# A hybrid decoder step on one Trainium2 core: the first delta chunk's gate rows, differences, exponentials and key products placed around the last projection tile

## The chip, the cores and the metric

The kernel runs as one launch on one core of a Trainium2 chip. The metric is device time in microseconds, from three executions of the kernel before. One more execution was taken with the hardware profiler, and all rows below are from that one.

## The reference, cut to what matters

The program is one inference step of a two-layer decoder trunk, for a prompt of 512 tokens and for 8 sequences of 4 sample tokens (544 columns in all). Each layer has three branches that read the same normalised input; branch A is a gated DeltaNet, and the change lies in it:

```python
c, dn_conv_new = _causal_conv(dn_qkv, dn_conv0, dn_conv_w)
q, k, v = jnp.split(jax.nn.silu(c), [DN_HEADS * DN_DK, 2 * DN_HEADS * DN_DK], axis=-1)
q = _l2norm(heads(q, DN_HEADS)) * DN_DK ** -0.5
k = _l2norm(heads(k, DN_HEADS))
beta = jax.nn.sigmoid(dn_b.astype(F32))
g = -jnp.exp(dn_a_log.astype(F32)) * jax.nn.softplus(dn_a.astype(F32) + dn_dt_bias.astype(F32))
o_a, dn_s_new = _chunked_recurrence(q, k, heads(v, DN_HEADS), g, beta, dn_s0)
```

In each chunk of the recurrence a unit lower-triangular system is solved. Its matrix is built from key products k k^T, from exponentials of differences of the running sums of g, and from beta. The output also needs the products k q^T with the same exponentials. Branch C is a sparse attention. Its sample part reads pages of a cache of keys and, once the probabilities are there, pages of a cache of values.

## The kernel before

The program is written engine by engine: each engine has one function with its instructions in the order in which they run, and semaphores tie the functions together. The same code is run for both layers, so what happens once in it happens twice in the profile. PSUM is split into two wide buffers `PJ[0]` and `PJ[1]` (`big` in the profile) and four banks `X[0]` to `X[3]` (`aux`). `claim` names the next use of a bank and gives the count of `drained` at which the bank is free again; `filled` says that TensorE has written it. All ScalarE operations go through one helper (L1564), so ScalarE's rows are told apart by their tiles.

Two phases matter here. The **projection phase** runs over `DN_PHASE`, 20 tiles p = 0 to 19. A tile is two halves of 8 k-steps with three matmuls each (`dense_tile`, L880 to L882), and in `between()` something may be placed between its halves. Tiles that carry q, k or v of the DeltaNet are then copied out by ScalarE into `d_pad` (with the stored rows), run through a convolution of four operations on VectorE (L2380, L2383) into `d_conv`, and through Silu on ScalarE into `qkv`. `silu_of(11)` is the last of these, for the tile p = 19. In the last tiles the sample attention ends as well: `sample_probabilities` (after p = 18, transposes at L942 into `X[2]`, `X[3]` and `X[0]`), and `new_values` (between the halves of p = 19, L1215, into `X[1]`), which ScalarE copies to `s_new` (the tile `s_ak` in the profile).

The **chunk phase** runs over five chunks, c = 0 to 3 with 128 tokens and c = 4 with the 32 sample tokens. TensorE begins a chunk with four groups of four matmuls: the gate rows `grow` into `X[1]` and `betarow` into `X[0]` (L1285), then the key products `kk` into `X[2]` and `kq` into `X[3]` (L1292). VectorE takes the differences `dif` from `grow` (L2434, into `d_dec`), ScalarE takes the exponential of `d_dec` and, from the bank of `grow`, the exponential `d_eg`, and VectorE goes on to the matrix of the system. TensorE meanwhile goes on with two value pages, the transposes `dvT` into `X[1]`, two more value pages, ten gate steps (a gate step is one k-step of a gate projection, placed here to fill waits), `dkT` and so on.

A value page is a DMA of 256 KB from the cache into one of four buffers. These buffers are the memory of `d_conv` and `d_pad`, so the SP queue waits for the last Silu before it issues the first:

```python
sp.wait_ge(act_out.sem, act_out.at(('silu', 11)))
for i in range(NPAGES):
    if i >= VPAGES:
        sp.wait_ge(pe_out.sem, pe_out.at(('v', i - VPAGES)))
    sp.dma_start(g.vpage[i % VPAGES], page('cache_v', *divmod(i, NPG)))...
```

Of the kernel before, what the change touches and what calls it, by code (L numbers as in the profile page):

```python
# [25 lines left out]
ALU = mybir.AluOpType  # L26
# [3 lines left out]
P = 128  # L30
# [7 lines left out]
H = 4  # L38
# [190 lines left out]
def gate_no(u, i):  # L229

    return int(u[4]) * 8 + int(u[5]) * 2 + i
# [427 lines left out]
def layer_program(g, layer):  # L659
# [218 lines left out]
    def _(pe):  # L878
# [330 lines left out]
        def new_values():  # L1209

            pe.wait_ge(X[0].drained, X[0].at('spT_new'))
            pe.wait_ge(X[1].drained, X[1].claim('s_new'))
            for h in range(H):
                hs = slice(h * NS, h * NS + NS)
                mm = pe.matmul(X[1].ap[hs, 0:P], g.s_pT[0:NS, NPG, hs], g.s_v[:, h * P:h * P + P], start=True, stop=True)  # L1215
            mm.then_inc(X[1].filled, 1)

        for p, (u, j) in enumerate(DN_PHASE):
            def between():
                key_slot(2 * p)  # L1220
                if p in L2_AT:
                    t = L2_AT[p]
                    column_sums(('l2', t), 1 - p % 2, [((lambda: pe.wait_ge(act_out.sem, act_out.at(('l2sq', t)))), g.l2)])
                if p == SELECT_AT:
                    repeat_selection(0)
                    repeat_selection(1)
                if p == SELECT_AT + 3:
                    new_values()
            dense_tile(('gate', gate_no(u, j)) if u in GATES else ('dn', 2 * int(u[2]) + j), p % 2, u, j, g.uhi, g.ulo,
                       between=between)  # L1230
            key_slot(2 * p + 1)
            if p == SELECT_AT:
                repeat_selection(2)
                new_keys()
            if p == SELECT_AT + 2:
                sample_probabilities()
        pe.wait_ge(PJ[0].drained, PJ[0].claim('so'))

# [38 lines left out]
        for c in range(5):  # L1277
            cs, n = chunk_of(c)
            tri = const('triu') if c < 4 else const('triu_s', NS)[:, 0:NS]
            q, k, v = (g.qkv[:, 4 * i:4 * i + 4, cs] for i in range(3))  # L1280
            for bank, key, src, rhs in ((X[1], 'grow', gG, tri), (X[0], 'betarow', gBeta, ident[0:n, 0:n])):
                pe.wait_ge(bank.drained, bank.claim((key, c)))
                x = bank.ap
                for h in range(H):
                    mm = pe.matmul(x[:, h * n:h * n + n], src[0:n, c, h:h + 1].to_broadcast([n, P]), rhs,  # L1285
                                   start=True, stop=True)
                mm.then_inc(bank.filled, 1)
            for bank, key, a, b in ((X[2], 'kk', k, k), (X[3], 'kq', k, q)):
                pe.wait_ge(bank.drained, bank.claim((key, c)))
                x = bank.ap  # L1290
                for h in range(H):
                    mm = pe.matmul(x[0:n, h * n:h * n + n], a[:, h, :], b[:, h, :], start=True, stop=True)  # L1292
                mm.then_inc(bank.filled, 1)
            if c == 4:
# [265 lines left out]
    def _(ac):  # L1560
# [255 lines left out]
        def silu_of(t):  # L1816
# [5 lines left out]
                    act_out.sem, act_out.next(('silu', t)))  # L1822
            ac.wait_ge(act_out.sem, act_out.count)
        ac.wait_ge(vec_out.sem, vec_out.at('d_pads'))
        even_pages(-1)
        for p, (u, j) in enumerate(DN_PHASE):
# [7 lines left out]
            if u in GATES:  # L1834
# [9 lines left out]
                continue  # L1844
            t = 2 * int(u[2]) + j
            pad = g.d_pad[t % 2]
            if t >= 2:
# [20 lines left out]
            if p == SELECT_AT + 1:  # L1868
# [3 lines left out]
                ac.wait_ge(act_out.sem, act_out.count)  # L1872
            if p == SELECT_AT + 3:
                copy_out(X[1], 's_new', lambda x: [(g.s_new, x[:, 0:P])])
        silu_of(11)
# [16 lines left out]
        for c in range(5):  # L1892
            cs, n = chunk_of(c)
            ac.wait_ge(vec_out.sem, vec_out.at(('dif', c)))
            act(g.d_dec[0:n, 0:4 * n], g.d_dec[0:n, 0:4 * n], ACT.Exp).then_inc(act_out.sem, act_out.next(('dec', c)))
            ac.wait_ge(act_out.sem, act_out.count)
            if c:
                ac.wait_ge(X[0].drained, X[0].at(('dS', c - 1)))
            copy_out(X[1], ('grow', c), lambda x: [(g.d_eg[:, 0:4 * n], x[:, 0:4 * n])], f=ACT.Exp)
            if c == 4:  # L1900
# [163 lines left out]
    def _(ve):  # L2064
# [264 lines left out]
        def sample_logits():  # L2329
# [18 lines left out]
            ve.wait_ge(vec_out.sem, vec_out.count)  # L2348

        odd_pages(-1)  # L2350
        for p, (u, j) in enumerate(DN_PHASE):
# [22 lines left out]
            if t is None:  # L2374
                continue
            ve.wait_ge(act_out.sem, act_out.at(('pad', t)))
            if t >= 2:
# [50 lines left out]
        for c in range(5):  # L2428
            cs, n = chunk_of(c)
            tri = const('triu') if c < 4 else const('triu_s', NS)[:, 0:NS]  # L2430
            ve.wait_ge(X[1].filled, X[1].at(('grow', c)))
            x = X[1].ap
            for h in range(H):
                ts(g.d_dec[0:n, h * n:h * n + n], x[0:n, h * n:h * n + n], gC[0:n, c, h:h + 1], 0.0,  # L2434
                        ALU.subtract, ALU.min).then_inc(vec_out.sem, vec_out.next(('dif', c) if h == 3 else None))
                ve.wait_ge(vec_out.sem, vec_out.count)
            ve.wait_ge(act_out.sem, act_out.at(('dec', c)))
# [355 lines left out]
```

## Time and profile before

| what | value |
|---|---|
| median of 3 runs | 3038.18 us (3035.11 to 3042.14) |
| profiled execution, its own time | 3036.19 us |
| profiled execution, span of the trace | 3034.3 us |
| mean granted TensorE clock | 0.955 |
| busy: TensorE, VectorE, ScalarE | 2817.3, 1620.5, 1177.2 us |

A busy time is the sum of an engine's instructions, and says nothing of what the others waited for. A row of the timeline gives the start of a group of like instructions, the time from its first start to its last end, the line, the tiles (output, then inputs) and how many they are. Square brackets hold the time in which that engine was idle just before, and the work that ended this idle time. A matmul of float32 operands in the groups of the chunk phase stands as two instructions, so four matmuls are counted as x8. PEclk 1.00 is TensorE's full clock of 2.4 GHz and 0.50 is 1.2 GHz. Ends of matmuls overlap the next start, so durations on TensorE are best read from start to start.

### The profile page before, as it was taken

The page shows a single profiled execution, that of the slowest core. Times are in us where ns is not written, and L with a number is a line of the kernel's source. Part 1 is how long each engine was busy: PE and PEld are TensorE (multiplying, and loading weights), DVE is VectorE, ACT ScalarE, POOL GpSimd, SP SyncE. Part 2 cuts the span into 40 slices and gives each one's busy share as a digit, 9 for nine tenths or more (in the row PEclk, how much of TensorE's full clock was granted, in tenths as well). Part 3 has the DMA queues.
Part 4 walks back from the last instruction along what each step waited for, and adds up shares of the span by engine and source line. Part 5 has one row for each costly group of instructions (what it writes and reads, how often), then busy time and mean ns, then how long its engine had stood idle before and what let it go on. Part 6 is the DMA issues. An engine that isn't in the chain of part 4 may idle for free. (4 is left out here: it accounts for less than half of the span.)

```text
span 3034.3 us, 56732 instructions
## 1 busy us (share of the span) xinstructions
PE 2817.3 (93%) x22451; PEld 2635.6 (87%) x22451; DVE 1620.5 (53%) x2513; ACT 1177.2 (39%) x2049; POOL 788.7 (26%) x364
## 2 busy tenths in 40 slices
PE   5998999998999799999979989999899979999998
PEld 4998888887887799999968989888888869999997
DVE  2363665564445549558225538546644464781861
ACT  3442333673223533333334315447622343432332
POOL 1221131221002333343322203222200124334431
PEclk8999899999999899999979979999999999999998
DMA  5221333534335432232242223255343344223323
GB/s 173 70 84 51 104 103 96 171 120 123 110 99 178 141 84 80 68 104 80 68 117 70 70 67 99 97 150 159 108 119 104 109 152 151 70 71 104 84 74 95
DMA packets 371700, 316.74 MB, mean 104 GB/s; under 512 B 47726, under 2 KB 321544, under 8 KB 370502
## 3 DMA queue, kind: packets, MB, share of 16 engines
q10 hardware_dynamic: 257332, 188.09, 20.9%
q1 hardware_dynamic: 114098, 124.96, 14.1%
q8 instruction: 181, 2.97, 0.4%
q14 instruction: 89, 0.73, 0.1%
HBM read 276.84 MB, written 36.15 MB: 103 GB/s over the span
## 5 line engine op out<-in xcount | busy, mean ns | idle before, releaser
L873 POOL TENSOR_TENSOR w_lo<-w_raw,w_hi 128x1024 fp32r<-128x1024 f32 (+2 forms) x360 | 788.5, 2194 | 2207.9 <-ACT w_hi L1564 2207.7
L880 PE MATMUL big<-uhi,w_hi 128*128 128x272 f32 x4096 | 1242.3, 303 | 54.0 <-DVE ulo L2084 31.9
L882 PE MATMUL big<-uhi,w_lo 128*128 128x272 f32 x4096 | 1200.6, 293 | 0.0
L881 PE MATMUL big<-ulo,w_hi 128*128 128x272 f32 x4096 | 1195.1, 292 | 0.0
L880 PEld LDWEIGHTS big<-uhi,w_hi 128*128 128x128 f32 x4096 | 788.5, 192 | 108.2 <-issue 60.1
L881 PEld LDWEIGHTS big<-ulo,w_hi 128*128 128x128 f32 x4096 | 789.9, 193 | 4.2 <-issue 1.9
L882 PEld LDWEIGHTS big<-uhi,w_lo 128*128 128x128 f32 x4096 | 787.5, 192 | 0.0
L1564 ACT ACTIVATE w_hi<-w_raw 128x1024 fp32r<-128x1024 f32 (+2 forms) x360 | 343.7, 955 | 425.1 <-PE big L882 329.5
L880 PE MATMUL big<-hhi,w_hi 128*128 128x272 f32 x704 | 205.9, 292 | 3.9 <-DVE hlo L2664 3.9
L882 PE MATMUL big<-hhi,w_lo 128*128 128x272 f32 x704 | 203.5, 289 | 0.0
L881 PE MATMUL big<-hlo,w_hi 128*128 128x272 f32 x704 | 202.7, 288 | 0.0
L1564 ACT ACT_TABLE_LOAD x106 | 136.0, 1283 | 41.7 <-PE big L931 14.3
L2670 DVE TENSOR_TENSOR x<-x,big 128x544 f32<-128x544 f32 x32 | 23.1, 722 | 236.2 <-PE big L882 236.2
L2403 DVE TENSOR_TENSOR d_T<-d_T,aux 128x512 f32<-128x512 f32 (+2 forms) x100 | 62.6, 626 | 144.5 <-PE aux L1342 143.1
L2646 DVE TENSOR_SCALAR f_conv<-f_pad,par 128x560 f32<-128x560 f32 x88 | 136.0, 1545 | 3.1
L880 PEld LDWEIGHTS big<-hhi,w_hi 128*128 128x128 f32 x704 | 132.8, 189 | 5.0 <-DVE hlo L2664 4.3
L881 PEld LDWEIGHTS big<-hlo,w_hi 128*128 128x128 f32 x704 | 132.8, 189 | 0.4
L882 PEld LDWEIGHTS big<-hhi,w_lo 128*128 128x128 f32 x704 | 132.3, 188 | 0.0
L2648 DVE SCALAR_TENSOR_TENSOR f_conv<-f_pad,par,f_conv 128x560 f32<-128x560 f32 x88 | 117.8, 1339 | 3.1
L2383 DVE SCALAR_TENSOR_TENSOR d_conv<-d_pad,par,d_conv 128x568 f32<-128x568 f32 x72 | 106.8, 1483 | 2.6
L1564 ACT ACTIVATE d_y<-aux 128x256 f32<-128x256 f32 (+2 forms) x102 | 38.9, 382 | 171.2 <-PE aux L1328 169.3
L1564 ACT ACTIVATE ffn_last<-f_pad 128x2 f32<-128x2 f32 (+1 forms) x176 | 37.1, 211 | 153.1 <-DVE f_pad L2642 150.0
(360 smaller groups left out, 3905.2 us busy)
## 6 DMA issues: line engine op xcount, KB each, us to landing
w_raw<-in_w_in ACTq DMA_DIRECT2D x66, 1024.0 KB, 5.6
w_raw<-in_w_up ACTq DMA_DIRECT2D x88, 512.0 KB, 5.0
kpage<-in_cache_k SPq DMA_DIRECT2D x128, 256.0 KB, 3.1
w_raw<-in_w_down ACTq DMA_DIRECT2D x32, 704.0 KB, 4.7
d_conv<-in_cache_v SPq DMA_DIRECT2D x64, 256.0 KB, 2.7
d_pad<-in_cache_v SPq DMA_DIRECT2D x64, 256.0 KB, 2.7
gate_dram<-gate_raw ACTq DMA_DIRECT2D x48, 272.0 KB, 2.5
w_raw<-in_w_branch ACTq DMA_DIRECT2D x24, 512.0 KB, 3.7
```

What stands on the lines that cost most here:

```text
L873: po.tensor_tensor(split_view(lo, t), tile_of(t), split_view(hi, t).bitcast(F32), ALU.subtract).then_inc(w_lo.sem, w_lo.next(t))
L880: pe.matmul(out, wh, xh, start=start, stop=False)
L881: pe.matmul(out, wh, xl, start=False, stop=False)
L882: return pe.matmul(out, wl, xh, start=False, stop=stop)
L1564: return ac.activation(out, in_, f, **kw)
L2383: stt(y, src[:, i:i + DW - 3], par('dc', i * 12 + t), y, ALU.mult, ALU.add).then_inc(vec_out.sem, vec_out.next(('conv', t) if i == 3 else ...
L2403: tt(d, d, bank.ap[0:n, at:4 * n], ALU.subtract).then_inc(bank.drained, 1)
L2646: ts(y, src[:, 0:SW - 2], par('f0', t), None, ALU.mult).then_inc(vec_steps.sem, vec_steps.next())
L2648: stt(y, src[:, 1:SW - 1], par('f0', 2 * FT + t), y, ALU.mult, ALU.add).then_inc(vec_steps.sem, vec_steps.next())
L2670: tt(halves(g.x[:, c, :]), halves(g.x[:, c, :]), x[:, :, 0:HT], ALU.add).then_inc(PJ[c % 2].drained, 1)
```

## The change

Of chunk 0, and of it alone, the four groups and what follows `grow` are placed earlier. `grow` stands after `sample_probabilities`, ahead of the tile p = 19. `betarow` and `kq` stand between the halves of that tile, behind `new_values`. `kk` stands behind the tile. VectorE's differences are ahead of the convolution of tile 19, and ScalarE's two exponentials are ahead of its copies of tile 19. `new_values` now writes `X[2]` in place of `X[1]`, and its copy to `s_new` stands right behind the exponentials rather than behind `silu_of(10)`. Chunks 1 to 4 keep their order. The code of the groups is moved into functions, which the diff shows without their unchanged bodies:

```diff
@@ TensorE
+        def gate_rows(c, bank, key):
+            ...
+        def key_products(c, bank, key):
+            ...
         for p, (u, j) in enumerate(DN_PHASE):
             def between():
...
                 if p == SELECT_AT + 3:
                     new_values()
+                    gate_rows(0, X[0], 'betarow')
+                    pe.wait_ge(vec_out.sem, vec_out.at(('l2', 7)))
+                    key_products(0, X[3], 'kq')
...
             if p == SELECT_AT + 2:
                 sample_probabilities()
+                gate_rows(0, X[1], 'grow')
+        key_products(0, X[2], 'kk')
         pe.wait_ge(PJ[0].drained, PJ[0].claim('so'))
...
+            if c:
+                gate_rows(c, X[1], 'grow')
+                gate_rows(c, X[0], 'betarow')
+                key_products(c, X[2], 'kk')
+                key_products(c, X[3], 'kq')
@@ ScalarE
+        def decays(c):
+            n = chunk_of(c)[1]
+            ac.wait_ge(vec_out.sem, vec_out.at(('dif', c)))
+            act(g.d_dec[0:n, 0:4 * n], g.d_dec[0:n, 0:4 * n], ACT.Exp).then_inc(act_out.sem, act_out.next(('dec', c)))
+            ...
+            copy_out(X[1], ('grow', c), lambda x: [(g.d_eg[:, 0:4 * n], x[:, 0:4 * n])], f=ACT.Exp)
...
+            if p == SELECT_AT + 3:
+                decays(0)
+                copy_out(X[2], 's_new', lambda x: [(g.s_new, x[:, 0:P])])
...
-            if p == SELECT_AT + 3:
-                copy_out(X[1], 's_new', lambda x: [(g.s_new, x[:, 0:P])])
@@ VectorE
+            if p == SELECT_AT + 3:
+                gate_steps_of(0)
             ve.wait_ge(act_out.sem, act_out.at(('pad', t)))
```

What this makes of the order on TensorE, around the middle of tile 19. Before, only the two rows of `new_values` (L1215) stand between the halves, and they wait for `X[1]`:

```order
L882 MATMUL big1<-uhi,w_lo0 128x272
L1215 MATMUL aux1<-s_v,s_pT 32x128 [waits aux1_drained,aux0_drained]
L1215 MATMUL aux1<-s_v,s_pT 32x128 x3
L880 MATMUL big1<-uhi,w_hi0 128x272
L881 MATMUL big1<-ulo,w_hi0 128x272
```

Now `betarow` (L1225) and `kq` (L1235) stand there too:

```order
L882 MATMUL big1<-uhi,w_lo0 128x272
L1215 MATMUL aux2<-s_v,s_pT 32x128 [waits aux2_drained,aux0_drained]
L1215 MATMUL aux2<-s_v,s_pT 32x128 x3
L1225 MATMUL aux0<-consts,gate 128x128 [waits aux0_drained]
L1225 MATMUL aux0<-consts,gate 128x128 x3
L1235 MATMUL aux3<-qkv 128x128 [waits aux3_drained,vec_made]
L1235 MATMUL aux3<-qkv 128x128 x3
L880 MATMUL big1<-uhi,w_hi0 128x272
```

The second half of the tile begins behind eight more matmuls, and the four of `grow` stand ahead of the tile in the same way.

TensorE again, from the last matmul of tile 19 to the first value page (loaded into `d_conv0`). Before:

```order
L882 MATMUL big1<-uhi,w_lo0 128x272
L1285 MATMUL aux1<-consts,gate 128x128 [waits aux1_drained,big0_drained]
L1285 MATMUL aux1<-consts,gate 128x128 x3
L1285 MATMUL aux0<-consts,gate 128x128 [waits aux0_drained]
L1285 MATMUL aux0<-consts,gate 128x128 x3
L1292 MATMUL aux2<-qkv 128x128 [waits aux2_drained]
L1292 MATMUL aux2<-qkv 128x128 x3
L1292 MATMUL aux3<-qkv 128x128 [waits aux3_drained]
L1292 MATMUL aux3<-qkv 128x128 x3
L1245 MATMUL big0<-d_conv0,s_pT 32x128 [waits v_page_loaded0]
```

Now:

```order
L882 MATMUL big1<-uhi,w_lo0 128x272
L1235 MATMUL aux2<-qkv 128x128 [waits aux2_drained]
L1235 MATMUL aux2<-qkv 128x128 x3
L1271 MATMUL big0<-d_conv0,s_pT 32x128 [waits v_page_loaded0,big0_drained]
L1271 MATMUL big0<-d_conv0,s_pT 32x128 x3
```

Of the 16 matmuls between the tile and the first value page four are left.

ScalarE at the start of chunk 1. Before, the exponential of `d_dec` stands right behind the last copy of chunk 0, and waits for the differences itself:

```order
L1564 ACTIVATE qkv<-aux 128x4x128 [waits aux3_filled]
L1564 ACTIVATE d_dec<-d_dec 128x512 [waits vec_made,aux3_drained]
L1564 ACTIVATE d_eg<-aux 128x512 [waits aux1_filled,aux0_drained,act_made]
L1564 ACTIVATE d_T<-aux 128x2x256 [waits aux2_filled,aux1_drained]
```

Now a load of the table of functions stands between them, with the wait for the differences on it:

```order
L1582 ACTIVATE qkv<-aux 128x4x128 [waits aux3_filled]
L1582 ACT_TABLE_LOAD [waits vec_made]
L1582 ACTIVATE d_dec<-d_dec 128x512 [waits aux3_drained]
L1582 ACTIVATE d_eg<-aux 128x512 [waits aux1_filled,aux0_drained,act_made]
```

The load that stood ahead of chunk 0's exponential is gone from there, since the last function before it is now an Exp; the first Exp behind the last Silu is now the one of chunk 1. The number of loads in the program is the same.

## Rows read from the trace of the kernel before

**Rows 1.** The page, part 1: busy us of an engine (share of the span) x instructions.

```profile
PE 2817.3 (93%) x22451; PEld 2635.6 (87%) x22451; DVE 1620.5 (53%) x2513; ACT 1177.2 (39%) x2049; POOL 788.7 (26%) x364
```

**Rows 2.** Stages of the five chunks, both layers: columns are span, busy time by engine, PEclk, DMA, GB/s.

```profile
711.00:911.00 200.00, 192.93 (x1833) 169.57 (x1831) 85.73 (x148) 48.58 (x94) 16.62 (x8) 0.99 0.37 108
2195.00:2396.00 201.00, 193.82 (x1837) 170.44 (x1835) 86.12 (x149) 49.44 (x96) 16.60 (x8) 0.99 0.36 107
```

**Rows 3.** Timeline of TensorE, layer 1: start us, us, engine line op, in brackets idle before it.

```profile
695.61 1.20 PE L942 MATMUL aux<-consts,s_log 128*128 128x128 f32 x9 [1.59 <-DVE s_log L2372]
696.57 0.37 PE L880 MATMUL big<-uhi,w_hi 128*128 128x272 f32 x1
...
699.75 0.42 PE L1215 MATMUL aux<-s_v,s_pT 32*32 32x128 f32 x8
...
703.09 0.29 PE L882 MATMUL big<-uhi,w_lo 128*128 128x272 f32 x1
...
709.03 3.75 PE L1285 MATMUL aux<-consts,gate 128*128 128x128 f32 x16 [5.65 <-ACT s_ak L1564]
712.58 3.00 PE L1292 MATMUL aux<-qkv 128*128 128x128 f32 x16
715.51 0.65 PE L1245 MATMUL big<-d_conv,s_pT 128*32 128x128 f32 x16
...
716.67 0.42 PE L1245 MATMUL big<-d_pad,s_pT 128*32 128x128 f32 x8
717.87 0.43 PE L1245 MATMUL big<-d_pad,s_pT 128*32 128x128 f32 x8 [0.78 <-DMA d_pad<-in_cache_v]
```

**Rows 4.** Timeline of TensorE, layer 2, the same place.

```profile
2193.86 3.75 PE L1285 MATMUL aux<-consts,gate 128*128 128x128 f32 x16 [5.65 <-ACT s_ak L1564]
...
2202.70 0.43 PE L1245 MATMUL big<-d_pad,s_pT 128*32 128x128 f32 x8 [0.55 <-DMA d_pad<-in_cache_v]
```

**Rows 5.** Timeline of ScalarE, layer 1.

```profile
696.40 1.51 ACT L1564 ACTIVATE s_pT<-aux 128x512 f32<-128x512 f32 x3
703.50 1.03 ACT L1564 ACTIVATE d_pad<-big 128x272 f32<-128x272 f32 x3 [5.59 <-PE big L882]
...
708.61 0.28 ACT L1564 ACTIVATE s_ak<-aux 128x128 f32<-128x128 f32 x1
709.99 0.89 ACT L1564 ACTIVATE qkv<-d_conv 128x512 f32<-128x512 f32 x2 [1.11 <-DVE d_conv L2383]
712.77 1.28 ACT L1564 ACT_TABLE_LOAD   x1 [1.89 <-DVE d_dec L2434]
714.07 0.63 ACT L1564 ACTIVATE d_dec<-d_dec 128x512 f32<-128x512 f32 x1
```

**Rows 6.** Timeline of VectorE, layer 1.

```profile
704.88 0.52 DVE L2380 TENSOR_SCALAR d_conv<-d_pad,par 128x568 f32<-128x568 f32 x1 [9.32 <-ACT d_pad L1564]
705.43 4.47 DVE L2383 SCALAR_TENSOR_TENSOR d_conv<-d_pad,par,d_conv 128x568 f32<-128x568 f32 x3
...
711.18 1.51 DVE L2434 TENSOR_SCALAR d_dec<-aux,gate 128x128 f32<-128x128 f32 x4 [0.63 <-PE aux L1285]
```

**Rows 7.** Timeline of the SP queue, layer 1: DMA issues.

```profile
711.64 1.43 SPq L802 DMA_DIRECT2D d_conv<-in_cache_v  x2
```

**Rows 8.** The first 5.57 us after the idle stretch, layer 1: columns as in rows 2.

```profile
709.03:714.60 5.57, 5.57 (x26) 5.57 (x27) 2.76 (x6) 2.68 (x4) 0.26 (x1) 0.50 0.47 132
```

**Rows 9.** Timeline of TensorE, layer 1, start of chunk 1.

```profile
761.50 2.09 PE L1285 MATMUL aux<-consts,gate 128*128 128x128 f32 x16
763.43 1.95 PE L1292 MATMUL aux<-qkv 128*128 128x128 f32 x16
765.31 0.64 PE L1245 MATMUL big<-d_conv,s_pT 128*32 128x128 f32 x16
765.88 0.66 PE L942 MATMUL aux<-consts,qkv 128*128 128x128 f32 x4
```

**Rows 10.** Timeline of ScalarE, layer 1, start of chunk 1.

```profile
764.93 0.60 ACT L1564 ACTIVATE d_eg<-aux 128x512 f32<-128x512 f32 x1
```

More of the change, by code:

```diff
@@ L1211, in new_values @@
             pe.wait_ge(X[0].drained, X[0].at('spT_new'))
-            pe.wait_ge(X[1].drained, X[1].claim('s_new'))
+            pe.wait_ge(X[2].drained, X[2].claim('s_new'))
             for h in range(H):
                 hs = slice(h * NS, h * NS + NS)
-                mm = pe.matmul(X[1].ap[hs, 0:P], g.s_pT[0:NS, NPG, hs], g.s_v[:, h * P:h * P + P], start=True, stop=True)
-            mm.then_inc(X[1].filled, 1)
+                mm = pe.matmul(X[2].ap[hs, 0:P], g.s_pT[0:NS, NPG, hs], g.s_v[:, h * P:h * P + P], start=True, stop=True)
+            mm.then_inc(X[2].filled, 1)
+        def gate_rows(c, bank, key):
+            n = chunk_of(c)[1]
+            tri = const('triu') if c < 4 else const('triu_s', NS)[:, 0:NS]
+            row, rhs = (gG, tri) if key == 'grow' else (gBeta, ident[0:n, 0:n])
+            pe.wait_ge(bank.drained, bank.claim((key, c)))
+            for h in range(H):
+                mm = pe.matmul(bank.ap[:, h * n:h * n + n], row[0:n, c, h:h + 1].to_broadcast([n, P]), rhs,
+                               start=True, stop=True)
+            mm.then_inc(bank.filled, 1)
+        def key_products(c, bank, key):
+            cs, n = chunk_of(c)
+            at = 4 if key == 'kk' else 0
+            pe.wait_ge(bank.drained, bank.claim((key, c)))
+            for h in range(H):
+                mm = pe.matmul(bank.ap[0:n, h * n:h * n + n], g.qkv[:, 4 + h, cs], g.qkv[:, at + h, cs],
+                               start=True, stop=True)
+            mm.then_inc(bank.filled, 1)
         for p, (u, j) in enumerate(DN_PHASE):
@@ L1280, in _ @@
             q, k, v = (g.qkv[:, 4 * i:4 * i + 4, cs] for i in range(3))
[L1281 to L1293, printed above, removed]
+            if c:
[3 more added lines that the diff above has]
+                key_products(c, X[3], 'kq')
             if c == 4:
@@ L1823, in silu_of @@
             ac.wait_ge(act_out.sem, act_out.count)
+        def decays(c):
+            n = chunk_of(c)[1]
+            ac.wait_ge(vec_out.sem, vec_out.at(('dif', c)))
+            act(g.d_dec[0:n, 0:4 * n], g.d_dec[0:n, 0:4 * n], ACT.Exp).then_inc(act_out.sem, act_out.next(('dec', c)))
+            ac.wait_ge(act_out.sem, act_out.count)
+            if c:
+                ac.wait_ge(X[0].drained, X[0].at(('dS', c - 1)))
+            copy_out(X[1], ('grow', c), lambda x: [(g.d_eg[:, 0:4 * n], x[:, 0:4 * n])], f=ACT.Exp)
         ac.wait_ge(vec_out.sem, vec_out.at('d_pads'))
@@ L1893, in _ @@
             cs, n = chunk_of(c)
-            ac.wait_ge(vec_out.sem, vec_out.at(('dif', c)))
-            act(g.d_dec[0:n, 0:4 * n], g.d_dec[0:n, 0:4 * n], ACT.Exp).then_inc(act_out.sem, act_out.next(('dec', c)))
-            ac.wait_ge(act_out.sem, act_out.count)
             if c:
-                ac.wait_ge(X[0].drained, X[0].at(('dS', c - 1)))
-            copy_out(X[1], ('grow', c), lambda x: [(g.d_eg[:, 0:4 * n], x[:, 0:4 * n])], f=ACT.Exp)
+                decays(c)
             if c == 4:
@@ L2348, in sample_logits, with gate_steps_of @@
             ve.wait_ge(vec_out.sem, vec_out.count)
+        def gate_steps_of(c):
+            n = chunk_of(c)[1]
+            ve.wait_ge(X[1].filled, X[1].at(('grow', c)))
+            x = X[1].ap
+            for h in range(H):
+                ts(g.d_dec[0:n, h * n:h * n + n], x[0:n, h * n:h * n + n], gC[0:n, c, h:h + 1], 0.0,
+                        ALU.subtract, ALU.min).then_inc(vec_out.sem, vec_out.next(('dif', c) if h == 3 else None))
+                ve.wait_ge(vec_out.sem, vec_out.count)
         odd_pages(-1)
@@ L2430, in _ @@
             tri = const('triu') if c < 4 else const('triu_s', NS)[:, 0:NS]
[L2431 to L2436, printed above, removed]
+            if c:
+                gate_steps_of(c)
             ve.wait_ge(act_out.sem, act_out.at(('dec', c)))
```

## The prediction

> **What bounds the kernel now.** I first read the page's busy times. TensorE is busy for 2817.3 us, 93% of the span [rows 1], so a change is worth what it does to TensorE's time. The stages of the chunk phase say the same of the place of the change: TensorE is busy for 192.9 of 200 us in layer 1 and for 193.8 of 201 in layer 2 [rows 2]. A delay at the phase's start therefore moves the whole phase; there is little idle time in it to absorb one.
>
> Then I read the timeline around the start of the phase. The last matmul of tile 19 starts at 703.09 and takes 0.29, so the tile ends at 703.38. TensorE is idle for 5.65 us and starts chunk 0's groups at 709.03 [rows 3]; layer 2 has the same gap [rows 4]. The release is ScalarE's copy of `s_new` (`s_ak`), which runs at 708.61 behind `silu_of(10)` and frees `X[1]` for `grow` [rows 5]. The groups then run at half clock, 0.50 over 5.57 us, which is 1.2 GHz [rows 8]: from 709.03 to 715.51 [rows 3], where chunk 1's take 3.81, from 761.50 to 765.31 [rows 9]. So there is an idle gap of 5.65 us and some 2.7 us of half-clock loss, and the change aims at both.
>
> The question is what ends last. Value page 3 (the fourth) starts at 717.87 and waits for its DMA, and so does its twin in layer 2 at 2202.70 [rows 3, 4]. In layer 2 the tile ends at 2193.86 - 5.65 = 2188.21. Both times page 3 starts 14.49 us after the end of tile 19. That is one chain: tile 19 ends at 703.38; ScalarE copies it to `d_pad` at 703.50 [rows 5]; VectorE convolves it from 704.88 to 705.43 + 4.47 = 709.90 [rows 6]; ScalarE runs the last Silu from 709.99 to 710.88 [rows 5]; the SP queue, which waits for that Silu, issues the first page at 711.64 [rows 7]; pages follow about 1.1 us apart (two in 1.43 us, each issue being about 0.33); page 3 lands at 717.87. TensorE's gap and its half-clock groups lie beside this chain. They cost nothing, except that the chain starts from the tile's end.
>
> **The change, part by part.**
>
> *Work put ahead of the tile's end.* `grow` stands before tile 19, `betarow` and `kq` in its middle. At full clock `grow` and `betarow` take 763.43 - 761.50 = 1.93 us, `kk` and `kq` 765.31 - 763.43 = 1.88 [rows 9]. The three groups moved ahead of the tile's end are 0.965 + 0.965 + 0.94 = 2.87 us. TensorE is dense from 695.61 to 703.38 [rows 3], with nothing to hide them. Tile 19 ends at 706.25, and everything on the chain follows: Silu ends at 713.75, SP issues at 714.51, page 3 can start at 720.74. **Cost 2.87 us per layer.**
>
> *The gap.* `kk` needs only that `s_new` is copied, which now happens by about 701.5. It runs from 706.25 to 707.2. Page 0 is issued at 714.51. I take its landing from page 3, issued some 3.3 us behind page 0 and landed at 717.87, so about 2.9 us from issue; page 0 lands near 717.4. So TensorE is idle for about 10 us instead of 5.65. The work that covered part of the wait is gone, and the wait is not.
>
> *Clock.* The gap of 5.65 us ended at 0.50, and 5.57 us of work passed before the full clock came back [rows 8]. The longer gap ends at half clock too. Before, the slow stretch lay under the wait for the pages; now it starts with page 0, near 717.4, and would last to about 723. Up to page 3 TensorE has only pages and `dvT` to do, so the loss there is page 3 itself, some 0.29 us of work at double length: 0.25. Behind it stand ten dense gate steps. Some 1.6 us of them fall into the slow stretch. Half clock stretches work by 3.55 / 1.93 = 1.84 (`grow` and `betarow`, 709.03 to 712.58, against rows 9) [rows 3, 9], so 1.6 us of it loses 0.7. **Cost 0.95 us per layer**, between 0 (clock back before page 3) and 0.25 + 5.57 x (1 - 1/1.84) = 2.8 (clock back only after as much dense work as it took before).
>
> *ScalarE's table load.* The load of 1.28 us ahead of chunk 0's Exp [rows 5] goes; that Exp now follows an Exp with only copies between. The load comes back ahead of chunk 1's Exp, behind the wait for the differences, as its row at 712.77 shows it placed. In chunk 1 `d_eg` ends at 764.93 + 0.60 = 765.53 [rows 10], and `dvT`, which needs `grow`'s bank free, starts at 765.88 [rows 9]. The slack is 0.35, so `dvT` starts 0.93 later plus a handover of about 0.06. **Cost 1.0 us per layer**; at least 0, if TensorE's later waits absorb it. VectorE's chain is pushed by the same 1.28, but its next operand, `dkT`, comes behind ten gate steps. The nearest row for the upper end is the idle time of 1.89 ahead of the load at 712.77 [rows 5]: if it belonged to the load and not to VectorE's differences, the load would cost 3.2 and the stall be 2.9.
>
> By the Trainium skill, "ScalarE: Activation LUTs", section "What ACT_TABLE_LOAD costs", a switch of tables costs about 2.66 us, the load and a drain behind it; the stall in chunk 1 would be 2.4 by that and the forecast 2.8 us later. The trace disagrees so far: the Exp starts at 714.07, 1.30 after the load's start.
>
> *Costed at nothing.* VectorE's differences (1.51) and ScalarE's two exponentials now run in the first half of tile 19, near 698 to 701; both engines were idle there, for 9.32 and 5.59 us [rows 5, 6]. If they ran late, ScalarE's `d_pad` copy would be held and the chain with it, but there are about 5 us to spare. Nothing of the gain in chunk 0's matrix counts either: TensorE asks for it only after ten gate steps. The swap of banks costs nothing, since `X[2]`, `X[3]` and `X[0]` are copied out by 697.91 [rows 5], before the middle of the tile.
>
> *Sum.* 2.87 + 0.95 + 1.0 = 4.8 us per layer, 9.6 for both. The profiled execution took 3036.19, so its twin should take 3045.8. It lies 2.0 below the median of 3038.18; on the median the forecast is **3047.8 us, 0.32% slower**. What a measurement of this kernel can tell from no change is about 0.2%, 6 us.
>
> **Rivals** (all on the median).
>
> - *The gap was the bound* (faster). If the pages were there when TensorE asks, it would run from the tile's end to the first gate step without a wait: 3.81 us of groups and about 1.9 of pages and `dvT`, 5.7 in place of the 14.8 it takes now. That is 9.1 per layer less 1.0 for the table load: 3022. For it speaks the plain row of 5.65 idle before L1285. Against it speaks the SP queue's wait for the last Silu. For any gain page 3 would have to start less than 14.49 - 2.87 - 1.0 = 10.6 us after the end of tile 19, where 14.49 stand in both layers. 7%. A rule of the Trainium skill would point this way ("TensorE: Matmul & The Clock Gate", section "HAM oscillation — how this bites in real kernels"): keep TensorE from waiting between stretches of work, since it goes back to its slow clock. No row here has these groups running behind the tile without a gap.
> - *Only the moved work counts* (no measurable change). The clock is back before the gate steps and chunk 1 absorbs the table load: 2 x 2.87 = 5.7, 3043.9, 0.19%. For it: pages and `dvT` keep TensorE busy for a while before the dense work. 20%.
> - *The clock stays low longer.* 2.87 + 2.8 + 1.0 = 6.7 per layer, 3051.5. For it: TensorE is only partly busy between pages. 12%.
> - *The table load costs more than its row*, with the stall of 2.9: 6.7 per layer as well, 3051.6. Against it stands the Exp's start right behind the load. 6%.
>
> The forecast has 55%. The range runs from 3041 (only the moved work, less the 3 us by which runs lie below the median) to 3054 (one of the two dearer cases, plus some run-to-run spread); it leaves out the faster case and the mixed tails. Faster by over 0.2%: 7%. Within 0.2%: 23%, the second rival and the low edge of the forecast. Slower by over 0.2%: 70%.
>
> **What the changed kernel's profile would show.** Tile 19's last matmul ends about 2.9 us later, counted from the transposes of `sample_probabilities`. Behind it come four matmuls and an idle stretch of about 10 us that a value page's DMA ends, not `s_ak`. Page 3 again starts 14.5 us after the tile's end. The clock is at 0.50 in the first gate steps. An ACT_TABLE_LOAD stands in chunk 1, and TensorE waits about 1 us there for ScalarE's `d_eg`. I am wrong if the first page lands sooner after tile 19 than now, or if the chunk phase as a whole gets shorter.

## The result, and the profile after

The changed kernel is slower: 3045.54 us in the median of 20 runs (3038.88 to 3050.15) against 3037.78 us for the kernel before, now with 20 runs as well (3031.62 to 3051.73). The ratio is 1.0024, 95% interval 1.0015 to 1.0032, so 7.3 us with an interval of 4.6 to 9.7 (the medians themselves differ by 7.8). The forecast was 9.6 us more, 3047.8 us, between 3041 and 3054. Here and below the ratios leave out executions over 1.5% above the fastest of their kernel: there were two, both of experiment 6, with 4518 and 5360 us against 3035 to 3044 for its other ten, and no trace shows what held them.

The page of the changed kernel, part 1:

```profile
PE 2809.3 (92%) x22451; PEld 2626.0 (86%) x22451; DVE 1621.0 (53%) x2513; ACT 1176.9 (39%) x2049; POOL 787.8 (26%) x364
```

TensorE is busy for 8 us less than before [rows 1] in a span that is longer. Some 2.7 us per layer of this are the groups, which no longer run at half clock; most of the rest comes from a place that the change doesn't touch (the stretch from 1600 to 1640 below). Less busy time is no gain here: idle time stands in its place, and more of it.

The timeline of TensorE in the changed kernel, layer 1, from the transposes of `sample_probabilities` to the transposes of `d_T` (L942, `d_T`), which follow `dkT` and two gate steps:

```profile
696.24 1.20 PE L942 MATMUL aux<-consts,s_log 128*128 128x128 f32 x9 [1.60 <-DVE s_log L2407]
697.28 1.06 PE L1225 MATMUL aux<-consts,gate 128*128 128x128 f32 x8
...
701.28 0.42 PE L1215 MATMUL aux<-s_v,s_pT 32*32 32x128 f32 x8
701.63 1.16 PE L1225 MATMUL aux<-consts,gate 128*128 128x128 f32 x8
702.62 1.06 PE L1235 MATMUL aux<-qkv 128*128 128x128 f32 x8
...
706.40 0.29 PE L882 MATMUL big<-uhi,w_lo 128*128 128x272 f32 x1
706.52 1.05 PE L1235 MATMUL aux<-qkv 128*128 128x128 f32 x8
...
717.62 0.65 PE L1271 MATMUL big<-d_conv,s_pT 128*32 128x128 f32 x8 [10.04 <-DMA d_conv<-in_cache_v]
719.01 0.65 PE L1271 MATMUL big<-d_conv,s_pT 128*32 128x128 f32 x8 [0.74 <-DMA d_conv<-in_cache_v]
719.60 1.12 PE L942 MATMUL aux<-consts,qkv 128*128 128x128 f32 x4
720.64 1.09 PE L1271 MATMUL big<-d_pad,s_pT 128*32 128x128 f32 x16
...
726.98 0.60 PE L942 MATMUL aux<-consts,d_T 128*128 128x128 f32 x4
```

All of it answers to [rows 3]. `grow` is at 697.28, right behind the transposes; `betarow` and `kq` at 701.63 and 702.62, between the halves; the tile ends at 706.69, and `kk` begins at once. The gap of 5.65 us that the copy of `s_ak` ended is gone. In its place stand 10.04 us of idle time that the DMA of value page 0 ends, and page 1 waits again, 0.74. Page 3 stands in one row with page 2 here, but the load of its weights, which TensorE does ahead of the matmuls, has a row of its own:

```profile
721.07 0.20 PEld L1271 LDWEIGHTS big<-d_pad,s_pT 128*32 128x32 f32 x8 [0.23 <-DMA d_pad<-in_cache_v]
```

It waits for its DMA too, and stands 721.07 - 706.69 = 14.38 us behind the tile's end, where it was 14.49 before. The chain is the one of before, leg by leg, on ScalarE and on the SP queue (rows of [rows 5, 7] after the change):

```profile
700.05 0.63 ACT L1582 ACTIVATE d_dec<-d_dec 128x512 f32<-128x512 f32 x1 [1.52 <-DVE d_dec L2381]
700.71 0.60 ACT L1582 ACTIVATE d_eg<-aux 128x512 f32<-128x512 f32 x1
701.83 0.28 ACT L1582 ACTIVATE s_ak<-aux 128x128 f32<-128x128 f32 x1 [0.52 <-PE aux L1215]
706.80 1.03 ACT L1582 ACTIVATE d_pad<-big 128x272 f32<-128x272 f32 x3 [4.70 <-PE big L882]
...
713.29 0.89 ACT L1582 ACTIVATE qkv<-d_conv 128x512 f32<-128x512 f32 x2 [1.41 <-DVE d_conv L2420]
```

```profile
714.93 1.43 SPq L802 DMA_DIRECT2D d_conv<-in_cache_v  x2
```

The exponentials ran at 700.05 and 700.71, well hidden. But the copy of tile 19 into `d_pad` starts at 706.80, which is 10.56 us after the transposes' start at 696.24; before, it was 703.50 - 695.61 = 7.89. So the tile's end is 2.67 us later. The last Silu and the first page follow: from the `d_pad` copy to the SP queue's first issue it is 714.93 - 706.80 = 8.13 us, and before it was 711.64 - 703.50 = 8.14 [rows 5, 7].

I measure each kernel from the transposes' start to that of the `d_T` transposes, because what a profiled execution gained or lost earlier is then left out. For this the ends of the kernel before are needed, which were not among its rows so far. Its timeline of TensorE, one row of layer 1 and two of layer 2:

```profile
723.31 0.60 PE L942 MATMUL aux<-consts,d_T 128*128 128x128 f32 x4
...
2180.44 1.20 PE L942 MATMUL aux<-consts,s_log 128*128 128x128 f32 x9 [1.60 <-DVE s_log L2372]
...
2208.13 0.60 PE L942 MATMUL aux<-consts,d_T 128*128 128x128 f32 x4
```

Before: 723.31 - 695.61 = 27.70 us in layer 1 [rows 3] and 27.69 in layer 2. After: 726.98 - 696.24 = 30.74, and in layer 2, by these rows,

```profile
2181.12 1.20 PE L942 MATMUL aux<-consts,s_log 128*128 128x128 f32 x9 [1.60 <-DVE s_log L2407]
...
2202.46 0.65 PE L1271 MATMUL big<-d_conv,s_pT 128*32 128x128 f32 x8 [10.01 <-DMA d_conv<-in_cache_v]
...
2211.80 0.60 PE L942 MATMUL aux<-consts,d_T 128*128 128x128 f32 x4
```

2211.80 - 2181.12 = 30.68. That is 3.04 and 2.99 us more per layer. The mean granted clock over the first 5.3 us from value page 0 on is 0.56, against 0.50 for the first 5.57 us of the groups in [rows 8]:

```profile
717.60:722.90 5.30, 4.54 (x43) 2.78 (x44) 0.47 (x1) 0.00 (x0) 0.00 (x0) 0.56 0.75 242
```

The third part of the loss comes in chunk 1. TensorE there (the groups, the pages and `dvT` of layer 1, then `dvT` of layer 2) and ScalarE in layer 1, which answer to [rows 9, 10]:

```profile
765.19 2.09 PE L1225 MATMUL aux<-consts,gate 128*128 128x128 f32 x16
...
769.00 0.64 PE L1271 MATMUL big<-d_conv,s_pT 128*32 128x128 f32 x16
770.55 0.66 PE L942 MATMUL aux<-consts,qkv 128*128 128x128 f32 x4 [0.91 <-ACT d_eg L1582]
...
2255.33 0.66 PE L942 MATMUL aux<-consts,qkv 128*128 128x128 f32 x4 [0.92 <-ACT d_eg L1582]
```

```profile
767.95 1.28 ACT L1582 ACT_TABLE_LOAD   x1 [1.50 <-DVE d_dec L2381]
769.24 0.63 ACT L1582 ACTIVATE d_dec<-d_dec 128x512 f32<-128x512 f32 x1
769.90 0.60 ACT L1582 ACTIVATE d_eg<-aux 128x512 f32<-128x512 f32 x1
```

The table load of 1.28 us stands ahead of the Exp, `d_eg` ends at 770.50, and `dvT` has waited 0.91 and 0.92 us for it. Here `dvT` starts 770.55 - 765.19 = 5.36 us after the groups (the first of these rows), against 765.88 - 761.50 = 4.38 before [rows 9]: 0.98 more. With the 3.04 and 2.99 this makes 4.0 us per layer, 8.0 for both, which lies inside the interval of the measured 7.3.

The profiled executions themselves differ by only 4.3 us in span (3034.3 and 3038.6). Most of the rest is in a place that the change doesn't touch. Columns are busy times by engine, then the granted clock, here 0.91, in the kernel before:

```profile
1600.00:1640.00 40.00, 38.11 (x261) 35.13 (x261) 19.44 (x25) 18.10 (x32) 9.85 (x4) 0.91 0.24 67
```

and after:

```profile
1600.00:1640.00 40.00, 38.11 (x287) 35.24 (x286) 20.66 (x28) 19.76 (x35) 9.88 (x5) 1.00 0.23 67
```

The kernel before happened to spend part of this stretch at half clock and the changed kernel did not; from about 1541 to 1637 the lag of the changed kernel fell from 3.7 to 0.9 us. One trace's span is therefore no measure of a change of this size; the runs and the local stretch are.

### The profile page after: what moved, and what is told of

It is laid out like the page before. It is cut to its first block and busy times, and to the rows that moved or that the text cites. A ratio compares the mean times of both kernels' runs of the same rounds, so it can differ in the third digit from the quotient of the medians.

```text
span 3038.6 us, 56734 instructions
## 1 busy us (share of the span) xinstructions
PE 2809.3 (92%) x22451; PEld 2626.0 (86%) x22451; DVE 1621.0 (53%) x2513; ACT 1176.9 (39%) x2049; POOL 787.8 (26%) x364
```

## The experiments

All ratios are against the kernel before on the same chip at the same time. The change itself was not run again there, so an experiment and the change are compared through two ratios. "Local" is the time from the transposes to the `d_T` transposes, above the kernel before's 27.70 and 27.69 us. "dvT" says whether chunk 1 still pays the 0.98 us. "To dvT" is the time from the transposes to the start of `dvT` in chunk 1, both layers together, above the kernel before's 70.27 us in each (765.88 - 695.61 in layer 1): it holds the local part, the 0.98 and what lies between. Both are read from the one profiled execution of each kernel.

| kernel | ratio (95%) | us in all | local, layer 1, 2 | dvT | to dvT |
|---|---|---|---|---|---|
| the change | 1.0024 (1.0015 to 1.0032) | +7.3 | +3.04, +2.99 | pays | +8.0 |
| 1 early copy of `s_new` alone | 1.0003 (0.9993 to 1.0012) | +0.9 | +1.49, +1.55 | no | +3.1 |
| 2 change, table loaded in idle time | 1.0027 (1.0017 to 1.0037) | +8.2 | +3.20, +4.50 | no | +8.3 |
| 3 change, only `grow` early | 1.0028 (1.0017 to 1.0039) | +8.5 | +2.11, +2.12 | pays | +6.2 |
| 4 change, gate steps ahead of pages | 1.0005 (0.9994 to 1.0016) | +1.5 | +0.20, +0.15 | pays | +3.3 |
| 5 before, early pages | 0.9983 (0.9974 to 0.9993) | -5.2 | -0.97, -1.03 | no | -2.0 |
| 6 change, early pages | 1.0007 (0.9998 to 1.0017) | +2.1 | -1.37, -1.56 | pays | -1.0 |
| 7 `grow` early, pages, gate steps | 0.9943 (0.9928 to 0.9958) | -17.3 | -8.86, -8.84 | no | -17.1 |
| 8 all groups late, pages, gate steps | 0.9960 (0.9947 to 0.9972) | -12.1 | -5.30, -5.29 | no | -10.4 |
| 9 change, clock kept up | 1.0032 (1.0019 to 1.0045) | +9.7 | +2.77, +4.18 | pays | +9.0 |
| 10 change, 1.9 us more work in tile 19 | 1.0040 (1.0026 to 1.0053) | +12.2 | +5.68, +5.53 | pays | +13.2 |

The columns "us in all" and "to dvT" come from different executions and agree to 3.2 us in every row, which is about half the width of the intervals. So what these kernels gain or lose is found in this stretch, and differences of 2 us are read from the traces, not from the ratios.

### 1. Is the gap itself the cost?

The kernel before with `new_values` in `X[2]` and its copy early:

```diff
-            pe.wait_ge(X[1].drained, X[1].claim('s_new'))
+            pe.wait_ge(X[2].drained, X[2].claim('s_new'))
@@ ScalarE, p = SELECT_AT + 3, ahead of the copies of tile 19
+            copy_out(X[2], 's_new', lambda x: [(g.s_new, x[:, 0:P])])
```

> The kernel before with one thing of the change: new_values writes X[2] and ScalarE copies it to s_new ahead of the copies of tile 19, so that X[1] is free when grow asks for it. All four groups stay behind tile 19. Theory (the chain from the end of tile 19 through the last Silu to the value pages sets the end): the idle 5.65 us before the groups vanish, TensorE waits some 7 us in front of value page 0 instead, page 3 starts 14.5 us after the tile's end as before, and the time is that of the kernel before or up to 2 us more for the clock (0 to +2 us in all). Rival (the wait for s_new was itself what cost): 5.6 us less in each layer, 11 us less in all.

The time did not change (1.0003). TensorE in layer 1:

```profile
702.70 1.95 PE L1285 MATMUL aux<-consts,gate 128*128 128x128 f32 x16
...
713.79 0.66 PE L1245 MATMUL big<-d_conv,s_pT 128*32 128x128 f32 x8 [7.36 <-DMA d_conv<-in_cache_v]
...
724.28 0.60 PE L942 MATMUL aux<-consts,d_T 128*128 128x128 f32 x4
```

The groups begin right behind the tile, at full clock, 3.7 us for all four. Nothing is gained: a wait of 7.36 us for the first page stands behind them. Removing both things that looked like the loss, the 5.65 us and the half clock, gave 1.49 us more locally, since the slow clock now falls on the gate steps (it is 0.50 until about 720.8, and they begin at 717.90). The rival, that the gap itself was the cost, asked for 11 us less; the interval ends at 2.1 us less. It is out.

### 2. The table load

```diff
         silu_of(11)
+        act(g.stat[:, 9:10], g.stat[:, 12:13], ACT.Exp).then_inc(act_steps.sem, act_steps.next())
```

The added operation's result is used by nothing.

> The changed kernel with one more ScalarE operation, an Exp of one column right behind the last Silu (its result is not used), so that the load of the exponential's table falls into idle time and not into chunk 1. Theory: dvT of chunk 1 no longer waits for d_eg (0.91 us idle in the changed kernel), so 1.8 us less than the changed kernel, about 6 us more than the kernel before. Rival (the later start of dvT is hidden somewhere behind it): the time of the changed kernel, 7.8 us more than before.

In chunk 1 the wait is gone:

```profile
765.47 2.09 PE L1225 MATMUL aux<-consts,gate 128*128 128x128 f32 x16
...
769.27 0.64 PE L1271 MATMUL big<-d_conv,s_pT 128*32 128x128 f32 x16
769.85 0.66 PE L942 MATMUL aux<-consts,qkv 128*128 128x128 f32 x4
```

`dvT` starts right behind the two pages, 4.38 us after the groups' start at 765.47, exactly as before the change. So the mechanism of this term is shown, and its size, 0.98 us. The time did not fall, though (1.0027 against the change's 1.0024), which is what the rival said. The profiled execution shows where the gain went, though not that it must go there: in each layer 0.3 us more passed between the `d_T` transposes and chunk 1, and layer 2 lost 1.5 us more than the change did ahead of them, where the clock stayed low for long:

```profile
2207.00:2215.00 8.00, 7.42 (x52) 5.95 (x53) 0.00 (x0) 0.00 (x0) 0.00 (x0) 0.57 0.61 200
```

In this execution the clock took most of what the load gave, and 2 us are below what these runs can tell apart. Of my two theories the time alone decides for neither.

### 3. Only grow ahead of the tile

```diff
                     new_values()
-                    gate_rows(0, X[0], 'betarow')
-                    pe.wait_ge(vec_out.sem, vec_out.at(('l2', 7)))
-                    key_products(0, X[3], 'kq')
...
+        gate_rows(0, X[0], 'betarow')
         key_products(0, X[2], 'kk')
+        key_products(0, X[3], 'kq')
```

> The changed kernel with betarow and kq put back behind tile 19, beside kk; only grow stays ahead of the tile, with VectorE's differences and ScalarE's exponentials where the change has them. Theory (work placed ahead of the tile's end is paid in full): the tile ends 1.9 us sooner in each layer than in the changed kernel, page 3 with it, so 3.8 us less than the changed kernel and about 4 us more than before. Rival (the loss comes from the longer idle stretch and the clock after it, not from the moved work): the time of the changed kernel.

The `d_pad` copy came 8.79 us after the transposes, 0.90 more than before where the change has 2.67. So the tile ended 1.77 us sooner, as expected, but locally only 0.93 of it arrived (2.11 against 3.04). The wait for the pages was 8.13 us instead of 10.04, and the first gate steps fell further into the slow clock. In the time nothing of it is seen: 1.0028, from 1.0017 to 1.0039, is the rival's result, and the 4 us above the kernel before that I expected (1.0013) lie outside the interval. In the trace the kernel is 1.8 us below the change to `dvT`, both layers together, where 3.8 us were expected. So the tile's end moved as the theory had it, and its worth was half of what the theory had: less work ahead of the tile's end and the clock behind it are not independent.

### 4. Work in the wait

```diff
+            if c == 0:
+                advance(gates, 10)
             if c < 4:
                 value_page(next(pages))
                 value_page(next(pages))
             turn(X[1], ('dvT', c), P, n, [v[:, h, :] for h in range(H)], P)
...
-                advance(gates, 10)
+                if c:
+                    advance(gates, 10)
```

> The changed kernel with chunk 0's ten gate steps moved from behind value page 3 to the place ahead of value page 0, that is into the 10 us in which TensorE waits for the first page. Theory: ten gate steps, 4.0 us at full clock, no longer stand behind the pages, and the idle stretch shrinks to about 6 us; dkT starts some 4 to 4.9 us sooner in each layer, so 8 us less than the changed kernel, the time of the kernel before within 2 us. Rival (the matrix of chunk 0 on VectorE and ScalarE then sets the end of the chunk's start): a gain of less than 4 us over the changed kernel.

The time is that of the kernel before, 1.0005, and 6 us below the change, where 8 us were expected. TensorE waits 5.58 us instead of 10.04, and the `d_T` transposes come 722.57 - 694.67 = 27.90 us after the first ones:

```profile
716.01 0.65 PE L1271 MATMUL big<-d_conv,s_pT 128*32 128x128 f32 x8 [5.58 <-DMA d_conv<-in_cache_v]
...
722.57 1.05 PE L942 MATMUL aux<-consts,d_T 128*128 128x128 f32 x4
```

That is 2.84 us less than the change in either layer, where the ten gate steps alone take 3.9 (718.23 to 722.12 in the kernel before). The rest went to the clock: the pages, `dkT` and the `d_T` transposes run at half clock (1.05 us for the last, 0.60 in the change).

### 5 and 6. The pages off the chain

Four buffers that are free at this time take the first four pages, so the SP queue need not wait for the Silu. In 6 `dvT` waits for the last Silu itself, which it reads:

```diff
+    def page_home(i):
+        return (g.d_y, g.d_kd, g.d_vb, g.d_kb)[i][:, :] if i < VPAGES else g.vpage[i % VPAGES]
...
-        sp.wait_ge(act_out.sem, act_out.at(('silu', 11)))
+        sp.wait_ge(X[3].filled, X[3].at(('slog', 1)))
         for i in range(NPAGES):
+            if i == VPAGES:
+                sp.wait_ge(act_out.sem, act_out.at(('silu', 11)))
@@ TensorE, in 6
+            if c == 0:
+                pe.wait_ge(act_out.sem, act_out.at(('silu', 11)))
             turn(X[1], ('dvT', c), ...
```

> The kernel before with the first four value pages of a layer loaded early: their buffers are d_y, d_kd, d_vb and d_kb, free at that time, and the SP queue issues them behind the last key page instead of behind the last Silu. Pages 4 and later stay as they are. Theory: page 3 no longer waits, and TensorE goes from the half-clock groups straight to the gate steps, 0.9 us sooner in each layer, 2 us less in all (0 to 4). Rival (pages alone set the end of the stretch): several us per layer, 8 or more in all.

> The changed kernel with the same early pages. dvT of chunk 0 reads the output of the last Silu, which the pages' own wait had covered, so it now waits for that Silu itself. Theory: the chain from tile 19 loses only its last leg, the page loads. The last Silu ends near 714, dvT starts there instead of 719.6, and the first gate steps run at half clock: 3 to 5 us less than the changed kernel in each layer, the time of the kernel before within 2.5 us. Rival (nothing but the loads' landing held TensorE): all of the 10 us of idle time goes, 12 us or more below the kernel before.

On the kernel before the pages were worth 0.97 and 1.03 us locally, and 5.2 us in the time (2.1 to 7.9). The local 2.0 lies just outside that interval; no row here explains the difference. On the changed kernel they were worth 4.4 and 4.6 us per layer in the traces, as the first theory had it, and about 5 us in the time (1.0007 against 1.0024). The rival of 6, that only the landing held TensorE, is out:

```profile
714.42 1.12 PE L948 MATMUL aux<-consts,qkv 128*128 128x128 f32 x4 [6.09 <-ACT qkv L1590]
...
722.74 0.60 PE L948 MATMUL aux<-consts,d_T 128*128 128x128 f32 x4
```

Behind the pages stands the next leg of the same chain, the last Silu, with 6.09 us of idle time.

### 7 and 8. The change without its cost, and what its idea is worth then

Experiment 7 joins 2, 3 and 6, and runs the four pages and the ten gate steps of chunk 0 ahead of `dvT`. Experiment 8 has the same pages and gate steps on the kernel of experiment 1, so everything of chunk 0 stands behind the tile. The order in chunk 0 in both:

```diff
             if c < 4:
                 value_page(next(pages))
                 value_page(next(pages))
+            if c == 0:
+                value_page(next(pages))
+                value_page(next(pages))
+                advance(gates, 10)
+                pe.wait_ge(act_out.sem, act_out.at(('silu', 11)))
             turn(X[1], ('dvT', c), P, n, [v[:, h, :] for h in range(H)], P)
```

Both kernels have all of these lines; value pages 2 and 3 and the gate steps no longer stand behind `dvT` in chunk 0.

> The change without its cost: only grow, the differences and the two exponentials stay ahead of or inside tile 19; betarow, kk and kq stand behind it; the first four value pages are loaded early and used at once; the ten gate steps run before dvT, which waits for the last Silu; and an unused Exp behind that Silu loads the table in idle time. Theory: from the tile's end TensorE has 8 us of work without a wait, the last Silu is done by then and the matrix of chunk 0 nearly so, and dkT starts near 713 instead of 722: 7 to 9 us less than the kernel before in each layer, a ratio of 0.993 to 0.996. Rival (VectorE's chain of chunk 0 becomes the bound and takes it back): 1 to 3 us per layer, a ratio of 0.998 or more.

> The same early pages and early gate steps on the kernel before with the early copy of s_new, so that all four groups, the differences and the exponentials of chunk 0 stand behind tile 19. It tells what placing grow and the exponentials early is worth once the pages are off the chain. Theory: VectorE reaches the matrix of chunk 0 about 2.7 us later than in the kernel with grow early (differences, table load and Exp behind the last convolution), so 5 to 7 us less than the kernel before in each layer, a ratio of 0.995 to 0.997, and slower than that kernel by 3 to 6 us. Rival (the early differences and exponentials are worth nothing): the same time as that kernel.

Experiment 7 is the fastest kernel of the study, 3017.41 us in the median of 6 runs, ratio 0.9943. TensorE in layer 1, and the stretch around it:

```profile
704.72 1.95 PE L1241 MATMUL aux<-qkv 128*128 128x128 f32 x16
...
707.27 0.40 PE L1276 MATMUL big<-d_kb,s_pT 128*32 128x128 f32 x8
...
711.60 0.65 PE L948 MATMUL aux<-consts,qkv 128*128 128x128 f32 x4
712.71 0.66 PE L948 MATMUL aux<-consts,qkv 128*128 128x128 f32 x4 [0.46 <-DVE d_mt L2490]
...
714.16 0.66 PE L948 MATMUL aux<-consts,d_T 128*128 128x128 f32 x4
```

```profile
703.00:716.00 13.00, 11.65 (x115) 10.53 (x115) 10.06 (x13) 7.78 (x15) 2.88 (x1) 1.00 0.44 126
```

From the tile's end to `dvT` there is no wait, and the clock holds 1.00 throughout. The only wait before the `d_T` transposes is 0.46 us for VectorE. In 8 TensorE waits for `d_eg`, that is for the differences, the table load and the Exp that still stand behind the last convolution:

```profile
714.95 1.94 PE L948 MATMUL aux<-consts,qkv 128*128 128x128 f32 x8 [2.97 <-ACT d_eg L1575]
...
718.04 0.60 PE L948 MATMUL aux<-consts,d_T 128*128 128x128 f32 x4
```

So with the pages out of the way the placing of `grow`, the differences and the exponentials, together with the unused Exp that keeps the table load out of chunk 1, is worth 3.56 and 3.55 us per layer locally and 6.7 us for both to `dvT`. Between the two ratios it is 5 us, but their intervals overlap (up to 0.9958 and from 0.9947): the size rests on one trace of each kernel.

### 9 and 10. The clock, and more of the suspected work

Experiment 9 adds 72 matmuls of 272 columns ahead of value page 0, whose result page 0 overwrites. Experiment 10 repeats the four matmuls of `kq` twice:

```diff
@@ 9
+        for i in range(72):
+            pe.matmul(PJ[0].ap[:, 0, 0:HT], g.uhi[:, i % KD, 0:P], g.uhi[:, i % KD, 0:HT], start=True, stop=True)
@@ 10
-            for h in range(H):
+            for h in list(range(H)) * (3 if (key, c) == ('kq', 0) else 1):
```

> The changed kernel with 72 matmuls of 272 columns, whose result is overwritten, in the idle stretch between kk and value page 0 (9 to 9.5 us of work in a wait of 10 us). Nothing that is needed is moved; only TensorE's clock is touched. Theory: the clock is at 2.4 GHz when page 0 lands, page 3 still starts 14.5 us after the tile's end, and the gate steps lose nothing: 0.4 to 1.2 us less than the changed kernel in each layer up to dkT, 1 to 2.5 us in all, so still 5 to 7 us above the kernel before. Rival (most of the loss is the clock): the time of the kernel before.

> The changed kernel with kq's four matmuls between the halves of tile 19 done three times over (eight matmuls more, 1.9 us at full clock, the same result). Theory: each us of work ahead of the tile's end is a us: tile 19, the last Silu and page 3 are 1.9 us later in each layer, 3.8 us more than the changed kernel, 11 to 12 us more than the kernel before. Rival (the stretch has room for it): the time of the changed kernel.

In layer 1 of experiment 9 the clock held until behind the gate steps (1.00 again from 720 to 725.3), and the local loss shrank from 3.04 to 2.77. The tile's end is 2.69 us later there, so with the full clock the moved work is all of the loss but 0.08. In layer 2 it grew to 4.18: the clock held through the filler and three waits for pages (1.11, 1.14 and 0.50 us) and fell as the dense gate steps began. Layer 1 has the like waits (1.05, 1.03 and 0.79) and no fall, and what made the difference is open. The first stretch with full clock, and the fall:

```profile
706.00:716.00 10.00, 9.02 (x74) 8.80 (x72) 8.81 (x11) 5.09 (x11) 2.89 (x1) 1.00 0.47 137
2212.00:2216.00 4.00, 4.00 (x20) 4.00 (x21) 0.00 (x0) 0.00 (x0) 0.00 (x0) 0.57 0.67 206
```

The time didn't fall (1.0032). So the clock is not the larger part of what the change costs, and filler work to hold it up bought nothing that shows. In experiment 10 `kq` is x24 instead of x8:

```profile
702.34 2.84 PE L1235 MATMUL aux<-qkv 128*128 128x128 f32 x24
```

The `d_pad` copy came 12.37 us after the transposes, 1.81 later than in the change; the local loss grew by 2.64 and 2.54 us, and the time by about 5 us over the change, though the two intervals overlap. Set beside experiment 3 the price comes out plainly: from there to here the tile ends 3.58 us later in layer 1 (8.79 against 12.37), and the local loss grows by 3.57 us, from 2.11 to 5.68; in layer 2 by 3.41. Between these two kernels a microsecond put ahead of the tile's end costs a microsecond, and there is no room for it. Step by step the clock blurs this: 0.93 us for 1.77 from experiment 3 to the change, 2.64 for 1.81 from the change to here.

## Why the prediction was right, point by point

- *What bounds this place.* Right. The chain from tile 19's end through the last Silu to the value pages is unchanged in length (8.13 against 8.14 us to the first issue), and TensorE's gap moved to its end. Page 3 stands 14.38 us behind the tile's end where 14.5 was forecast, and waits for its DMA. Experiment 1 took the old gap away without gain, and experiment 6 moved the wait one leg up the same chain.
- *Moved work, 2.87 us.* The tile ended 2.67 us later in both layers. The mechanism is shown in the traces: by experiments 3 and 10, in which the tile ended 0.90 and 4.48 us later and the local loss differs by 3.6 and 3.4, and by layer 1 of experiment 9, where the clock held and this term alone was left. The runs alone don't show it, since experiment 3 was not faster than the change. The term was 0.2 too large: a group cost 0.89 us there, where I had taken 0.96 from chunk 1.
- *The gap.* Predicted about 10 us, measured 10.04 and 10.01 (717.62 and 2202.46).
- *Clock, 0.95 us.* The size was off. What is left of the local loss after the moved work is 3.04 - 2.67 = 0.37 and 0.32 us. After page 0 at 717.62 the clock was back 4.6 us later, near 722.2 (it is 0.50 for 0.88 of the stretch shown above), where the prediction had it slow to about 723. The gate steps began at 721.66, so about 0.6 us of them were slow, not 1.6. Among the experiments that keep the order behind the pages the same remainder lay between 0.08 (9, layer 1) and 1.81 (2, layer 2). The bounds 0 to 2.8 held; the middle value is not something that the kernel fixes.
- *Table load, 1.0 us.* Measured 0.98; the row at 712.77 gave the right size. The rival of a dearer load, and with it the 2.66 us of the Trainium skill ("ScalarE: Activation LUTs", section "What ACT_TABLE_LOAD costs"), does not show: in chunk 1 too the Exp of `d_dec` starts 1.29 after the load's start, 769.24 - 767.95. ScalarE was idle ahead of this load; in experiment 2 the load follows the last Silu at once (714.05, behind 713.14 + 0.89), and the next operation starts at 715.35, 1.30 behind it, so nothing hides ahead of the load either.
- *Costed at nothing.* The differences and exponentials were done by 701.31, 5.5 us ahead of the `d_pad` copy. Right.
- *The sum.* 4.0 us per layer instead of 4.8; measured 7.3 in all where 9.6 stood. The term that was mis-sized is the clock, 0.95 for a measured 0.35; 0.2 came from the moved work.
- *The rivals.* "The gap was the bound" is out by experiment 1. The rule of the Trainium skill behind it ("TensorE: Matmul & The Clock Gate", section "HAM oscillation — how this bites in real kernels"), to keep TensorE from waiting, paid only where real work took the wait's place (4 and 7), not where the clock alone was held up (9). "Only the moved work counts" is out by the waits of 0.91 and 0.92 in chunk 1; its 5.7 us lie inside the interval nonetheless, so the ratio alone does not decide between this rival and the forecast; the traces do. "The clock stays low longer" did not happen in the profiled run of the change, but something like it did in layer 2 of experiments 2 and 9.

## What to carry to other kernels

An idle gap is worth only what ends after it: before filling one, follow the chain that starts at the same point as the work you would move, and see which wait ends last. Here work was moved from beside a chain to ahead of it, and what had been free cost 2.67 us per layer. Take the last leg off the chain first (here, four free buffers and a later reader's own wait); then the same early placement, cut to what the next engine needs, was worth 3.5 us per layer in the traces. And when an Exp moves across a Silu, look for where the table load turns up.

## What the runs showed of the hardware that I had not expected

After an idle stretch the time to the full clock differed: 4.6 us after page 0 in the change (idle for 10.04 before), 7.0 in experiment 1 (idle for 7.36). The clock also fell where TensorE had not been idle. In the kernel before, five microseconds at full busy time, with no idle time in the 30 us ahead of them, have a mean clock of 0.75:

```profile
1610.00:1615.00 5.00, 5.00 (x28) 4.42 (x28) 2.70 (x5) 0.45 (x2) 0.68 (x1) 0.75 0.00 0
```

The clock had been 0.50 from 1580 to 1585 and full again from 1590 on. The changed kernel runs the same instructions some 3 us later and has 1.00 from 1600 to 1640. For changes of a few us this is an uncertainty as large as the effect: the lag of the changed kernel behind the kernel before fell by 2.8 us over a stretch of some 95 us that the change doesn't touch.
